# Turning the rows of a rotary embedding by transfers inside SBUF instead of by TensorE products, in a two-block transformer kernel

## What is computed

```python
# first block, layer l (x and the context stream xc)
q, k, v, up, ca, cb = project_inputs(modulate(rms_norm(x, g1), sh1, sc1), w_in[l], q_norm_g[l], k_norm_g[l])
q, k = apply_rope(q, cos, sin), apply_rope(k, cos, sin)      # x only; pairs (0, 1), (2, 3), ...
attn = diff_attention(q, concat(kc, k), concat(vc, v), lam)  # 4 heads, 2 maps each
conv_o = conformer_conv(ca, cb, ...)                         # 31 taps
x = x + g1 * (concat(attn, pool_o, conv_o) @ w_out[l])
x = x + g2 * swiglu(modulate(rms_norm(x, g2n), sh2, sc2), w_ffn_in[l], w_ffn_out[l])

def apply_rope(x, cos, sin):
    x1, x2 = x[..., 0::2], x[..., 1::2]
    return stack([x1 * cos - x2 * sin, x1 * sin + x2 * cos], -1).reshape(x.shape)

# second block, layer l
c_q, c_kv, k_r, q_d, k_d, v_d = split(rmsnorm(x, attn_norm[l]) @ w_in[l])
o_a = mla_mixer(c_q, c_kv, k_r, cos, sin, ...)   # 8 heads of 64 + 32; rotary on the 32, by halves
o_b = dilated_attention(q_d, k_d, v_d, rel_bias)
x = x + concat(o_a, o_b) @ w_out[l]
x = x + conv_ffn(rmsnorm(x, ffn_norm[l]), ...)

def apply_rope_2(x, cos, sin):
    x1, x2 = split(x, 2, axis=-1)
    return concat([x1 * cos - x2 * sin, x2 * cos + x1 * sin], -1)
```

## Time and profile before

| | |
|---|---|
| time, three runs | 1646.7, 1647.05, 1649.31 us |
| the profiled execution | 1644.55 us, of which its span is 1642.8 us |
| TensorE clock granted, mean over the span | 0.995 |
| PE, DVE, ACT, POOL busy | 97%, 69%, 56%, 8% |
| moved by DMA | 303.36 MB, mean 185 GB/s |
| L1575 tmp,cst 128*128 x 512 columns | 60 instructions |

### The profile page before, as it was taken

How to read it: one execution, slowest core, us unless ns; L and a number is a source line. 1 busy time by engine, 2 the same in 40 slices (tenths; PEclk the granted TensorE clock), 3 DMA queues, 4 the chain that set the end, 5 groups by cost and what they waited for, 6 DMA issues and landing times. The chain is left out here.

```text
span 1642.8 us, 31046 instructions
## 1 busy us (share of the span) xinstructions
PE 1589.0 (97%) x12874; PEld 1463.2 (89%) x12874; DVE 1129.8 (69%) x1763; ACT 919.0 (56%) x1459; POOL 127.2 (8%) x106
## 2 busy tenths in 40 slices
PE   6999999999999999999999999999999999999999
PEld 3987478999999999966899999878999998799999
DVE  2799677645566655897765556778887567788873
ACT  3444756545365444647554446767666467676662
POOL 0230000112001100300011000000101000001110
PEclk9999999999999999999999999999999999999999
DMA  9443666656546555435566653323555533245553
GB/s 395 160 152 131 258 236 227 235 216 240 192 167 221 205 188 201 155 125 207 195 228 237 220 184 119 118 78 130 207 191 202 204 112 116 77 137 200 207 193 118
DMA packets 46172, 303.36 MB, mean 185 GB/s; under 512 B 5072, under 2 KB 7376, under 8 KB 12752
## 3 DMA queue, kind: packets, MB, share of 16 engines
q1 hardware_dynamic: 45312, 299.78, 50.7%
q0 software_dynamic: 288, 0.92, 0.1%
q10 hardware_dynamic: 432, 0.68, 0.1%
HBM read 298.22 MB, written 3.15 MB: 183 GB/s over the span
## 5 line engine op out<-in xcount | busy, mean ns | idle before, releaser
L2002 DVE TENSOR_TENSOR wl<-raw,wh 128x1040 fp32r<-128x1040 f32 (+1 forms) x472 | 576.4, 1260 | 295.8 <-ACT wh L1759 229.9
L1759 ACT ACTIVATE wh<-raw 128x1040 fp32r<-128x1040 f32 (+1 forms) x472 | 466.5, 1031 | 195.5 <-PE bank L1552 109.3
L1547 PE MATMUL bank<-hx_hi,wh 128*128 128x256 f32 x1856 | 519.6, 280 | 6.0 <-ACT hx_hi L1759 3.8
L1552 PE MATMUL bank<-hx_lo,wh 128*128 128x256 f32 x1856 | 516.2, 278 | 0.0
L1550 PE MATMUL bank<-hx_hi,wl 128*128 128x256 f32 x1856 | 514.7, 277 | 0.3 <-DVE wl L2002 0.2
L1547 PEld LDWEIGHTS bank<-hx_hi,wh 128*128 128x128 f32 x1856 | 349.0, 188 | 10.8 <-issue 9.8
L1550 PEld LDWEIGHTS bank<-hx_hi,wl 128*128 128x128 f32 x1856 | 349.1, 188 | 2.8 <-issue 1.7
L1552 PEld LDWEIGHTS bank<-hx_lo,wh 128*128 128x128 f32 x1856 | 348.8, 188 | 1.0 <-DVE hx_lo L1995 0.4
L1550 PE MATMUL bank<-hid_hi,wl 128*128 128x256 f32 x912 | 252.2, 277 | 1.4 <-DVE wl L2002 1.4
L1547 PE MATMUL bank<-hid_hi,wh 128*128 128x256 f32 x912 | 252.5, 277 | 0.3 <-ACT wh L1759 0.2
L1552 PE MATMUL bank<-hid_lo,wh 128*128 128x256 f32 x912 | 251.9, 276 | 0.0
(11 more groups left out here) (218 smaller groups left out, 1891.5 us busy)
## 6 DMA issues: line engine op xcount, KB each, us to landing
raw<-in_wts SPq DMA_DIRECT2D x208, 1032.0 KB, 4.9
raw<-in_wts SPq DMA_DIRECT2D x50, 1024.0 KB, 6.6
raw<-in_wts SPq DMA_DIRECT2D x20, 776.0 KB, 4.3
raw<-in_wts SPq DMA_DIRECT2D x4, 584.0 KB, 4.4
tscr<-tmp SPq DMA_DIRECT2D x4, 512.0 KB, 7.4
bias<-tscr SPq DMA_DIRECT2D x4, 512.0 KB, 6.0
raw<-in_wts SPq DMA_DIRECT2D x2, 648.0 KB, 4.0
xTc<-in_ctxT SPq DMA_DIRECT2D x1, 1024.0 KB, 10.6
```

Of the source, the lines that this page charges most:

```text
L1547: pe.matmul(out, block(f, M.wh, w0 + k, ncols, c, m), x_hi, start=first and k == 0 and o == 0, stop=False, skip_group_check=True)
L1552: ins = pe.matmul(out, block(f, M.wh, w0 + k, ncols, c, m), x_lo, start=False, stop=last and k == nk - 1, skip_group_check=True)
L1759: return act.activation(out, in_, func, bias=bias, scale=scale)
L2002: tt(M.wl[k][:, cols], M.raw[r][:, cols], M.wh[k][:, cols].bitcast(F32), ALU.subtract).then_inc(*on.inc(lo))
```

## The change

The swap products are gone, and with them the two swap matrices. `cst` has three matrices. Behind `hn1` (and behind `lora1`) a new step `swap` makes ACT wait for the activation that wrote the rows and for the buffer they go to, and issue two transfers from SBUF to SBUF: each row is copied to the place of its partner. `PAIRS` exchanges even and odd rows (64 rows of 2 KB in each transfer), `HALVES` rows 64 to 79 and 80 to 95 (16 rows of 2 KB, of 1 KB in the lora part). The minus sign is in the tables of sines. The scratch tile `y` is taken when the rows are made, no longer in `rest`; `hn2` and `qn2` take one bank fewer, and in the lora part the turned rows go to the second half of `xg`. DVE has as many instructions as before: in `hn2` the multiply by the sines works in place; in `qn2` the multiply by the cosines goes first, writes the result and doesn't wait for the turned rows, and the multiply by the sines and the add cover rows 64 to 95 only. POOL's memset is gone.

```diff
-    sq = np.concatenate([c[k] for k in ("ident", "ones", "bones", "swap1", "swap2")], axis=1)
+    sq = np.concatenate([c[k] for k in ("ident", "ones", "bones")], axis=1)
...
-        cst = sb("cst", [P, 5 * P])
+        cst = sb("cst", [P, 3 * P])
...
+PAIRS = ((slice(0, P, 2), slice(1, P, 2)), (slice(1, P, 2), slice(0, P, 2)))
+HALVES = ((slice(64, 80), slice(80, 96)), (slice(80, 96), slice(64, 80)))
...
+    def turned_rows(rows, src, dst, ready, free):
+        t = [ev(f"swap{n_turn[0]}", 16) for _ in range(2)]
+        n_turn[0] += 1
+        step("swap", rows=rows, src=src, dst=dst, ready=ready, free=free, t=t)
+        return t[-1]
...
         banks.give(b, t_xg)
+        if swap:
+            y = tmps.get()
+            t_r = turned_rows(PAIRS, xg.t[:, :], y.t, t_xg, y.free)
...
+            t_sw = turned_rows(HALVES, xg.t[:, 0:T], xg.t[:, T:2 * T], k_g, [])
...
+            y = tmps.get()
+            t_r = turned_rows(HALVES, xg.t[:, :], y.t, t_xg, y.free)
...
         mm(s.t[0:np_, :], blk, sq.t[0:np_, :], True, True).then_inc(*on.inc(t_s))
-        if swap is not None:
-            on.wait_ge(t_xg, r_free)
-            mm(r.t[0:np_, :], swap, xg.t[0:np_, :], True, True).then_inc(*on.inc(t_r))
...
-        on.wait_ge(t_xg, r_free)
-        mm(r.t[0:96, :], M.swap2[0:96, 0:96], xg.t[0:96, :], True, True).then_inc(*on.inc(t_r))
...
-        on.wait_ge(z, k_g)
-        mm(br.t[0:96, 0:T], M.swap2[0:96, 0:96], xg.t[0:96, 0:T], True, True).then_inc(*on.inc(t_sw))
...
+    def swap(rows, src, dst, ready, free, t):
+        on.wait_ge(ready, free)
+        for (to, frm), t_i in zip(rows, t):
+            act.dma_start(dst[to, :], src[frm, :]).then_inc(*on.inc(t_i, 16))
...
-        on.wait_ge(t_r, t_tab, y_free)
-        tt(v(y.t), v(r.t), wide(S), ALU.mult).then_inc(*on.inc(t_d[0]))
+        on.wait_ge(t_r, t_tab)
+        tt(v(y.t), v(y.t), wide(S), ALU.mult).then_inc(*on.inc(t_d[0]))
...
+        on.wait_ge(t_xg, t_tab, out_free)
+        tt(o, v(xg.t), wide(M.ropeC), ALU.mult).then_inc(*on.inc(t_d[0]))
+        on.wait_ge(t_r)
+        tt(v(y.t, 64), v(y.t, 64), wide(M.ropeS, 64), ALU.mult).then_inc(*on.inc(t_d[1]))
+        on.wait_ge(t_d[1])
+        tt(o[64:96, :, :], o[64:96, :, :], v(y.t, 64), ALU.add).then_inc(*on.inc(t_d[2]))
...
-    def lora1(xg, xg_free, z, **_):
-        on.wait_ge(xg_free)
-        pool.memset(xg.t[0:64, 0:T], 0.0).then_inc(*on.inc(z))
```

More of the change, by code:

```diff
@@ L97, in shape_constants @@
     cs = np.cos(ang.astype(np.float64))[:, dim].T
-    sn = np.sin(ang.astype(np.float64))[:, dim].T
+    sn = np.sin(ang.astype(np.float64))[:, dim].T * np.where(np.arange(P) % 2, 1.0, -1.0)[:, None]
     rc = np.zeros((P, 2, T))
@@ L218, in __init__ @@
         b1_off = cur[0]
-        self.ident, self.ones, self.bones, self.swap1, self.swap2 = (
-            cst[:, P * i:P * i + P] for i in range(5))
+        self.ident, self.ones, self.bones = (
+            cst[:, P * i:P * i + P] for i in range(3))
         self.V = lambda k: vec[:, VT[k][0]:VT[k][0] + VT[k][1]]
@@ L632, in heads_norm @@
         banks.give(b, t_xg)
+        if swap:
+            y = tmps.get()
+            t_r = turned_rows(PAIRS, xg.t[:, :], y.t, t_xg, y.free)
         def rest():
             s, t_s = banks.get(), ev("mm")
-            r, t_r = (None, None) if swap is None else (banks.get(), ev("mm"))
-            s_free, r_free = s.free, r and r.free
+            s_free = s.free
             tmps.give(sq, t_s)
@@ L641, in rest @@
             banks.give(s, t_ln)
[L642 to L652, removed]
+            t_d = [ev("rope") for _ in range(4 if swap else 1)]
+            step("hn2", s=s, s_free=s_free, sq=sq, t_sq=t_sq, xg=xg, t_xg=t_xg, rs=rs, rs_free=rs_free,
+                 y=y if swap else None, blk=blk, tables=tables, nfeat=nfeat, np_=np_, out=out, out_free=out_free, t_s=t_s,
+                 t_r=t_r if swap else None, t_ln=t_ln, t_rs=t_rs, t_d=t_d)
+            tmps.give(xg, t_d[2 if swap else 0], t_r if swap else None)
+            if swap:
                 tmps.give(y, t_d[-1])
@@ L1237, in lora_norm @@
             kq.extend(tmps.get() for _ in range(2))
[L1238 removed]
+            a3, k_sq, k_g = [ev("lsq") for _ in range(3)], [ev("lsq"), ev("lsq")], ev("lsq")
             step("lora1", l=l, bk=(ba, bb, bc), tk=(ta, tb, tc), sq3=sq3, sq_free=[q.free for q in sq3], xg=xg,
[L1240 removed]
+                 xg_free=xg.free, a3=a3, kq=kq, kq_free=[q.free for q in kq], k_sq=k_sq, k_g=k_g)
+            t_sw = turned_rows(HALVES, xg.t[:, 0:T], xg.t[:, T:2 * T], k_g, [])
             kq_use.extend([t] for t in k_sq)
             def rest():
[L1244 to L1246 removed]
+                nq, nkv, rq, rk = banks.get(), banks.get(), None, None
+                tq, tkv = ev("mm"), ev("mm")
+                bfree = flat([nq.free, nkv.free])
                 tmps.give(sq3[0], tq)
@@ L1303, in latent_norm @@
             banks.give(b, t_xg)
+            y = tmps.get()
+            t_r = turned_rows(HALVES, xg.t[:, :], y.t, t_xg, y.free)
             def rest():
[L1306 to L1310, removed]
+                s_ = banks.get()
+                t_s, t_ln, t_rs, t_d = ev("mm"), ev("ln"), ev("rs"), [ev("rope") for _ in range(3)]
+                step("qn2", u=u, s=s_, s_free=s_.free, sq=sq, t_sq=t_sq, xg=xg, t_xg=t_xg, y=y, t_tab=list(t_rope),
+                     out_free=flat([rf, qs_free]), t_s=t_s, t_r=t_r, t_ln=t_ln, t_rs=t_rs, t_d=t_d)
                 tmps.give(sq, t_s)
                 banks.give(s_, t_ln)
-                banks.give(r, t_d[0])
-                tmps.give(xg, t_d[2])
+                tmps.give(xg, t_d[1], t_r)
                 tmps.give(y, t_d[2])
```

64 lines of the change are left out of this document (24 added, 40 removed).

## The result

The changed kernel takes 1656.78 us (median of 4; 1654.88 to 1657.33), the kernel before 1647.24 (4 runs). The ratio is 1.0054, with a 95% interval of 1.0043 to 1.0066: 9 us slower, 11.8 above the forecast of 1645.0 and outside the range that ended at 1652. The profiled execution took 1654.88 us, its span 1653.0.

A forecast was written before the change was run, and what follows sets the result against it. PE is 97% busy, but removed work pays only where PE is last at the engines' next meeting. Start 0.3, layer 0 1.5, layer 1 -0.4, block two 0.6: 2.0 us gained, 1645.0 from 1647.05; range 1639.5 to 1652.

The forecast's parts named there:

- What is removed: Swap products of both blocks and the lora part: 14.6 us of PE work, the ceiling of the gain.
- DVE: Rotary multiply by the sines reads SBUF instead of PSUM, in block two on 32 rows of 96: no change.
- The start: Constants shrink from 320 to 192 KB ahead of PE's first product: 0.3 us gained, bounds 0 and 1.3.
- Layer 0 of block one: PE's lead of 3.44 us fills DVE's idle of 2.07, less 0.5 for a late landing: 1.5 us gained.
- Layer 1 of block one: PE's 3.44 us become longer waiting at 739.84; one issue delays a weight piece's activation: 0.4 us lost.
- What is added on ACT: Behind each activation making the rows, two issues of 0.46 us plus the wait: 1.0 us a pair, 18 pairs.
- Block two: Per layer, (a) to (c) together: 0.3 us gained, 0.6 for both layers, bounds -3 and +6.
- (a): Lora swap of each block two layer: ACT 1.0 us late ahead of a head's root, 0.5 us lost.
- (b): Swaps 1 and 2 of a block two layer: issues fit ACT's idle of 1.05 us, PE keeps about 0.9.
- (c): Last two swaps of a block two layer: two pairs delay the copy at 1079.23; PE leaves with +0.6 us.
- Rival (5): ACT becomes the link in block two, pairs cost 1.3 us, four paid a layer: 1652 us, chance 0.13.
- The queues: Transfers between SBUF rows land in 2.0 us, bounds 1.7 and 5.4; only layer 0's slack of 2.75 is short.

The follow-up runs named there:

- e1: Changed kernel without the 36 transfers and ACT's wait for them, so rows are not exchanged: 1646.85 us, 1.0000 of the kernel before.
- e7: Changed kernel with block one's 16 transfers on ACT's queue and block two's 20 on POOL's: 1646.39 us, 0.9994 of the kernel before.
- e9: e7 plus three unread PE products ahead of the score products in each layer of block two: 1644.83 us, 0.9989 of the kernel before.
- e10: e7 plus unread PE products at six places where PE idles, in both blocks: 1641.11 us, 0.9965 of the kernel before.
- e12: Changed kernel, ACT's pairs in both blocks, plus unread PE products at the six places of e10: 1654.38 us, 1.0037 of the kernel before.
- e8: Changed kernel with all 36 transfers on SP's queue, which otherwise issues the weight pieces: 1647.64 us, 1.0000 of the kernel before.
- e6: Kernel before with transfers in block two only, each cut in two by columns (same bytes, four issues per swap): 1672.38 us, 1.0151 of the kernel before.
- e4: Changed kernel with all 36 transfers issued by POOL in place of ACT: 1649.93 us, 1.0018 of the kernel before.

## Why the prediction was wrong

**What is removed: right as a sum of work, and a term missing behind it.** 14.6 us as a ceiling stands, and so does the argument that little of it becomes time, since PE meets other engines. What I left out is the clock: e1 had 14.6 us less work, 7.1 less busy time, 7.2 more idle time and nothing less in the end, and lost some 8 us of full clock more. The table of the profile has the clock of 0.995, and the prediction no term for it.

**DVE: right as a median, and wrong at two places where it was put at nothing.** The multiply takes 0.686 us (median, L2061) from SBUF and 0.682 on 32 rows (L2075). But in layer 1 of block one two rotary multiplies take 1.2 us, and in block two the new order of `qn2` makes DVE's way to `k` 0.35 us longer, as shown above. The first place in the kernel before, then in the changed one:

```profile
692.20 0.68 DVE L2065 TENSOR_TENSOR tmp<-bank,rope 128x512 f32<-128x512 f32 x1
...
693.51 1.12 DVE L2068 TENSOR_TENSOR tmp<-tmp,tmp 128x512 f32<-128x512 f32 x1
```

```profile
692.44 1.22 DVE L2061 TENSOR_TENSOR tmp<-tmp,rope 128x512 f32<-128x512 f32 x1
693.59 1.23 DVE L2062 TENSOR_TENSOR tmp<-tmp,rope 128x512 f32<-128x512 f32 x1
```

The add behind them takes 0.69. It is the one of the eight rotations beside which POOL computes (its last pooling instruction runs to 694.3); at the other seven the multiplies take 0.68 to 0.69 us. e1, whose multiply also reads SBUF, has the same two durations. That POOL is what slows them is argued from this and not shown by a run of its own.

**The start: right for PE's first product, but not kept.** PE's first product starts at 8.90 instead of 9.22 us:

```profile
8.90 3.57 PE L1573 MATMUL bank<-raw,csil 128*32 128x512 f32 x16 [8.90 <-DMA cst<-in_csq]
```

By 30 us the changed kernel is 1.0 us late: a half-clock stretch now lies at 16 us (in the kernel before the first is at 29).

**Layer 0 of block one: right as a mechanism, 0.2 us off.** From 82 to 161 us the changed kernel gains 1.7 us; I had 1.5, from the idle of 2.07 us, which shrinks to 0.37:

```profile
154.10 1.12 ACTq L1815 DMA_DIRECT2D tmp<-tmp  x2
...
157.66 0.69 DVE L2061 TENSOR_TENSOR tmp<-tmp,rope 128x512 f32<-128x512 f32 x1
...
171.36 0.76 DVE L1991 SCALAR_TENSOR_TENSOR pcx<-bank,pcx 128x256 f32<-128x256 f32 x2 [0.37 <-PE bank L1573]
```

The landing that I feared at 156.75 isn't seen: the multiply follows its predecessor directly. With this slack it hung by little: in e7, e9, e10 and e12 the multiply waits 1.3 to 2.0 us for the transfer there, though nothing behind it is later for it. About 1.0 us of the gain is given back until 228 us, around a half-clock stretch at 207 us that lasts 6.8 instead of 3.4 us.

**Layer 1 of block one: the number right, the reason wrong, so this was luck.** Expected -0.4, seen -0.6 (0.23 at 690, 0.86 at 943). The pair behind 684.15 delays the weight piece's activation of the earlier trace rows by 1.54 us, and DVE now idles 0.71 us for it:

```profile
684.86 1.12 ACTq L1815 DMA_DIRECT2D tmp<-tmp  x2
686.03 2.02 ACT L1750 ACTIVATE wh<-raw 128x1040 fp32r<-128x1040 f32 x2 [1.20 <-issue]
...
687.19 3.01 DVE L1998 TENSOR_TENSOR wl<-raw,wh 128x1040 fp32r<-128x1040 f32 x2 [0.71 <-issue]
```

But these two instructions of DVE end where they would have ended, 3.01 us after they start instead of 3.80, and the delay is gone. DVE is 0.22 us late on either side of them. e1, which has no pair there, is as late as the changed kernel from 697 us on, 0.9 us both. The 0.7 us come between, in the rows above: the two multiplies take 1.1 us more, and the add 0.4 less. PE's wait at 739.84, which I expected to grow by 3 us, is 1.89 us instead of 1.62; another of 0.80 us appears ahead of it.

**What is added on ACT: the step that failed.** I took an issue at 0.46 us, from an issue at the start, when ACT did nothing, and the wait for its own result at 0.1. In place, an issue is 0.6 to 0.7 and a pair costs 1.3 to 1.6 us of ACT's order. 1.0 was "near" 1.05, the idle ahead of the root, as the prediction said; at 1.5 the idle doesn't cover it.

**Block two: wrong by that term, and by its sum.** Per layer the prediction had (a) 0.5 lost at the lora swap; measured 1.3 (0.86 to 2.15). (b) 0.9 gained by 1077 us; measured 0.9 lost (2.15 to 3.06). (c) 0.3 to 0.6 lost or gained at the last two swaps; measured 1.7 lost (3.06 to 4.77), with PE waiting 2.92 us for the copy. Of the last 1.7, 1.2 are the wait for DVE's `k`, which e1 and e10 have too. 3.9 us lost in the first layer where I had 0.3 gained. Rival (5) was the one that came true: pairs of 1.3 us, four of them paid, 1652. I gave it 0.13, and it was still 5 us too low. Its price was near, 5.2 us a layer against the 5.4 that the changed kernel lost against e1. Too high was what it let come back: 1.7 us of PE in each layer, where e1 gains 1.5 in the first and nothing in the second, and 1.8 before block two, where 0.9 were lost. The second layer loses 5.3, 1.4 more than the first, and has 6.8 us at half clock from 1415 us on.

**The queues: of no weight in the changed kernel, but not within my bounds.** 2.9 us for 128 KB (median; I had 2.0, bounds 1.7 and 5.4) and 2.0 for 32 KB; five landed in 6.2 to 7.8 us, all within their slacks. The prediction's sentence that a landing of 5.1 us leaves every slack but the one of 2.75 us intact was wrong by its own numbers: with 0.9 for the issues, the slack of 4.6 us is short too. The Trainium skill (DMA: Bandwidth & Descriptors, "Issuing engines are not separate DMA queues") says that transfers interleave with others on the same engines, whoever issued them. The trace agrees: 1.9 to 2.1 us for 128 KB alone, 2.8 to 7.8 beside weight pieces; it cost no time here. Its sentence that another issuing engine only saves the time on the sequencer, usually small beside the transfer, is borne out by e7 and e8 as far as the saving goes, only that this time, 1.2 to 1.4 us a pair against 2 us of landing, is what mattered here.

## What to carry to other kernels

Moving work from the engine that is 97% busy to one that is 56% busy pays only if the second engine is free at that place: look at who waits next behind each inserted instruction, and price it with its wait for its own engine's last result. Here a pair of issues whose operand was long ready ran beside the activation in front of it and was nearly free; the same pair directly behind the activation that makes its operand cost 1.3 to 1.6 us of ACT's order. Work removed from a busy engine mostly becomes waiting at the next engine that it meets: follow its lead to that meeting before you count it. And when PE gets less to do, look at the granted clock: part of the gained time can be given back as slower products, and products that nobody reads, placed in PE's waits, kept most of it (0.9965 of the kernel before against 0.9994). Last, an engine that issues a transfer does so in its own order: POOL's pooling held a pair back by 9 us.

## What the runs showed of the hardware

- An issue on ACT's queue took 0.41 to 0.46 us at the start and 0.47 to 0.64 us in a pair within the changed kernel (once 0.85, once 1.66; single issues of other runs up to 1.58); for 8 KB (e6) it took as long as for 128 KB. On POOL's queue a pair took 1.08 us (e4) and the landing was no slower (medians 2.4 us for 128 KB, 1.8 for 32 KB), on SP's 2.2 and 2.0 us (e8).
- A transfer of 128 KB between partitions of SBUF, in rows of 2 KB, landed in 1.9 to 2.1 us on ACT's queue with nothing else in flight and in 2.8 to 7.8 us beside weight pieces.
- DVE's rotary multiplies of 128 x 512 with both sources in SBUF took 0.68 to 0.69 us at seven of eight places. At the one where POOL was computing they took 1.22 and 1.23 us (changed kernel and e1); in the kernel before the multiply from a bank took 0.68 there, the one from SBUF 0.68 and the add 1.12.
- PE with 14.6 us less work lost 19 instead of 11.5 us of full clock (means over the runs of e1 and of the kernel before). With unread products in its waits the kernel before came to a mean of 0.998 in its profiled execution.
